# Two decoder blocks on one core: the embedding product, the gates and the stick attention in another order

## The reference

```
h = h + 0.5 * swiglu(rmsnorm(h, ffn2_norm), w_gate, w_up, w_down)     # "MLP 2"
gate = sigmoid(rmsnorm(h, ple_gate_norm) @ ple_w_gate)                 # 1024 x 1024
emb  = rmsnorm(p @ ple_w_proj, ple_norm)                               # p is 512 x 256: does not depend on h
h = h + gate * emb

mem_attention(rmsnorm(x), rmsnorm(mem, norm_mem), ...)                 # mem is 256 x 1024

# stick breaking, per head, strictly causal
z = q @ k.T / 8
log_beta, log_1m = log_sigmoid(z), where(strict, log_sigmoid(-z), 0)
tail = reverse_cumsum(log_1m) - log_1m
out = where(strict, exp(log_beta + tail), 0) @ v
```

## Time and profile before

| | |
|---|---|
| median of 3 executions | 2682.81 us |
| profiled execution | 2682.83 us, span 2680.9 |
| TensorE matmul busy | 2611.9 us (97%) |
| VectorE busy | 1567.8 us (58%) |
| ScalarE busy | 909.2 us (34%) |
| mean granted TensorE clock | 0.99 |
| load of a slab, issue to landing | 4.8 us |
| chain that ended last | 90% TensorE, 7% VectorE, 2% ScalarE |

### The profile page before, as it was taken

The page is one execution under the profiler, slowest core; times in us unless marked ns, Lnnn a source line. Parts: engine busy times, 40 slices in busy tenths (PEclk is TensorE's granted clock), DMA queues, the critical chain, the costliest instruction groups (busy, mean ns, idle before and its releaser), DMA issues.

```text
span 2680.9 us, 32197 instructions
## 1 busy us (share of the span) xinstructions
PE 2611.9 (97%) x12690; PEld 2140.0 (80%) x12690; DVE 1567.8 (58%) x1934; ACT 909.2 (34%) x1186; POOL 0.2 (0%) x4
## 2 busy tenths in 40 slices
PE   8999999989999999998999999999999999999999
PEld 6888887768888877876888888888886789888887
DVE  6444456676444468477555766566346656574745
ACT  4222243544212134434342423234136343432322
POOL 0000000000000000000000000000000000000000
PEclk9999999999999999999999999999999999999999
DMA  5222232003322222211322222323210132122222
GB/s 176 95 94 94 94 121 80 32 33 103 109 86 102 94 94 89 101 64 63 110 96 78 96 97 92 108 81 129 95 64 1 63 126 95 64 95 96 102 100 79
DMA packets 36596, 240.68 MB, mean 90 GB/s; under 512 B 3952, under 2 KB 6912, under 8 KB 8320
## 3 DMA queue, kind: packets, MB, share of 16 engines
q1 hardware_dynamic: 35008, 234.12, 25.4%
q10 hardware_dynamic: 1472, 4.94, 0.5%
HBM read 236.94 MB, written 2.10 MB: 89 GB/s over the span
## 4 chain that ended last, share of the span: by engine, by line
PE 90%; DVE 7%; ACT 2%; issue 1%; DMA 0%; SPq 0%; DVEq 0%; ACTq 0%
PE ps L474 24%; PE ps L476 24%; PE ps L475 24%; PE ps L1061 1%; PE ps L492 1%; PE ps L491 1%; PE ps L490 1%; PE ps L1007 1%; PE ps L502 1%; PE ps L1046 1%; PE ps L587 1%; DVE w_lo L1712 1%; PE ps L589 1%; PE ps L588 1%; PE ps L1072 1%
## 5 line engine op out<-in xcount | busy, mean ns | idle before, releaser
L474 PE MATMUL ps<-op_hi,w_hi 128*128 128x512 f32 x2128 | 841.3, 395 | 20.5 <-DVE op_lo L1626 14.5
L475 PE MATMUL ps<-op_lo,w_hi 128*128 128x512 f32 x2128 | 831.3, 391 | 0.0
L476 PE MATMUL ps<-op_hi,w_lo 128*128 128x512 f32 x2128 | 831.2, 391 | 0.0
L1115 ACT ACTIVATE w_hi<-w_raw 128x2048 fp32r<-128x2048 f32 x217 | 414.2, 1909 | 515.0 <-PE ps L476 355.3
L1712 DVE TENSOR_TENSOR w_lo<-w_raw,w_hi 128x2048 fp32r<-128x2048 f32 x217 | 497.1, 2292 | 50.6 <-ACT w_hi L1115 35.2
L474 PEld LDWEIGHTS ps<-op_hi,w_hi 128*128 128x128 f32 x2128 | 401.5, 189 | 111.8 <-issue 20.5
L475 PEld LDWEIGHTS ps<-op_lo,w_hi 128*128 128x128 f32 x2128 | 401.6, 189 | 87.5 <-issue 4.4
L476 PEld LDWEIGHTS ps<-op_hi,w_lo 128*128 128x128 f32 x2128 | 401.4, 189 | 84.2
L1677 DVE SCALAR_TENSOR_TENSOR x<-ps,x 128x512 f32<-128x512 f32 x134 | 92.6, 691 | 338.6 <-PE ps L476 320.9
L474 PE MATMUL ps<-h_hi,w_hi 128*128 128x512 f32 x692 | 273.4, 395 | 0.0
L476 PE MATMUL ps<-h_hi,w_lo 128*128 128x512 f32 x692 | 273.4, 395 | 0.0
(11 more groups left out here) (293 smaller groups left out, 3002.3 us busy)
## 6 DMA issues: line engine op xcount, KB each, us to landing
w_raw<-in_wstream_dram SPq DMA_DIRECT2D x217, 1024.0 KB, 4.8
w_raw<-in_wstream_dram SPq DMA_DIRECT2D x8, 256.0 KB, 7.9
x<-in_x_dram SPq DMA_DIRECT2D x4, 512.0 KB, 7.6
cr_m<-in_mem_dram ACTq DMA_DIRECT2D x2, 1024.0 KB, 4.7
out_dram<-x SPq DMA_DIRECT2D x3, 512.0 KB, 2.7
ev_s<-in_alibi_dram ACTq DMA_DIRECT2D x1, 1024.0 KB, 4.9
m_c<-in_rope_dram ACTq DMA_DIRECT2D x1, 704.0 KB, 4.3
pl_p<-in_p_dram ACTq DMA_DIRECT2D x1, 512.0 KB, 3.6
```

The source lines that it names most:

```text
L474: mm_(o, w_hi[:, c % 4, w], hi[:, k, 0:cols], start=(k == 0), stop=False)
L475: mm_(o, w_hi[:, c % 4, w], lo[:, k, 0:cols], start=False, stop=False)
L476: mm = mm_(o, w_lo[:, c % 4, w], hi[:, k, 0:cols], start=False, stop=(k == kt - 1))
L1115: f_(w_hi[:, c % 4, :], w_raw[:, c % 2, :], ACT.Copy).then_inc(w_hi_ready, 1)
```

## The change

- The embedding slab moves ahead of MLP 2's last four down slabs (`AT_EMB`), in the weight stream too. Its tiles go round five banks. ScalarE squares each tile in its bank and copies it to `pl_e` (`emb_kept`); VectorE copies only the eighth. Its row sum stands behind the first down slab. Embedding tiles 4 to 7 are scaled between down slabs, 0 to 3 between gates.
- A gate bank is freed when VectorE has scaled it, and the sigmoid waits for that. The last gate slab is made by halves. The order of the even mixer's norm is written out by tile.
- Memory's row sum stands behind the second slab of the even mixer's projection; `high(...+5)` goes ahead of `rs_mem`.
- Stick attention works in three units per pair, each with a pair of banks of its own: unit 0 is blocks 3 and 2 (384 columns), unit 1 block 1 (384), unit 2 block 0 (512). ScalarE and VectorE handle a unit with one instruction where they had one per block. Unit 0's buffers alternate between two sets. Units 0 and 1 of pair 0 are scored before the last value slab. The output takes blocks from 3 to 0 and waits per block. The projection's operand 0 to 6 is cut once the last exponent is made, and the eighth straight from its bank.

```diff
@@ TensorE
-            def mlp(at):
+            def embeddings(c):
+                start_slab(c)
+                pe.wait_ge(p_cut, 2)
+                for o in range(KT):
+                    if o >= 5:
+                        pe.wait_ge(emb_kept, o - 4)
+                    ...
+                    mm.then_inc(emb_done if o < KT - 1 else slab_done, 1)
+            def mlp(at, emb=False):
...
+                        if emb and d == 0:
+                            sum_rows(columns=False)
...
+                if emb:
+                    embeddings(AT_EMB)
...
-                    if memory and d == 0:
+                    if memory and d == 1:
                         sum_rows(MEM)
...
-            for d in range(1, DOWN):
-                to_features(AT_PLE + 1 + d, last=(d == DOWN - 1))
+            for d in range(1, DOWN - 1):
+                to_features(AT_PLE + d)
+            by_halves(AT_PLE + DOWN - 1, KT, gate_half, op_hi, op_lo, last=True)
...
+            def stick_scores(t, u):
+                if t:
+                    pe.wait_ge(a_made, 3 * (t - 1) + u + 1)
+                for kb in UNITS[u]:
+                    ...
+            stick_scores(0, 0)
+            stick_scores(0, 1)
+            to_positions(AT_ODD + ODD_SLABS - 1)
+            pe.wait_ge(acc_free, AT_ODD + ODD_SLABS + 1)
             for t in range(PAIRS):
-                stick_exponent(t, 3)
-                stick_scores(t, 1)
-                stick_scores(t, 0)
+                if t:
+                    stick_scores(t, 1)
+                stick_scores(t, 2)
                 if t:
                     stick_out(t - 1)
-                stick_exponent(t, 2)
+                stick_exponent(t, 0)
                 stick_exponent(t, 1)
                 if t < PAIRS - 1:
-                    stick_scores(t + 1, 3)
-                    stick_scores(t + 1, 2)
-                stick_exponent(t, 0)
+                    stick_scores(t + 1, 0)
+                stick_exponent(t, 2)
@@ ScalarE
+                if emb:
+                    high(AT_EMB + 3)
+                    for o in range(KT):
+                        ...
+                        square_sum(emb_bank(o))
+                        if o < KT - 1:
+                            f_(pl_e[:, o, :], emb_bank(o), ACT.Copy).then_inc(emb_kept, 1)
+                    high(AT_EMB + 4)
+                    high(AT_EMB + 5)
+                    inverse_rms_x(rs_emb, None)
+                    high(AT_EMB + 6)
...
+            for k in range(4):
+                act.wait_ge(gated_x, k + 1)
+                square_sum(x[:, k, :])
+            high(AT_EVEN + 2)
+            gate(KT - 2)
+            for k in range(KT - 1):
+                n["used"] += 1
+                act.wait_ge(op_used, n["used"])
+                if k == KT - 2:
+                    gate(KT - 1)
+                if k >= 4:
+                    act.wait_ge(gated_x, k + 1)
+                mixer_high(k)
...
             high(AT_EVEN + EVEN_SLABS + 4)
+            high(AT_EVEN + EVEN_SLABS + 5)
             inverse_rms_x(rs_mem, rs_col[:, NB:NB + 2])
-            high(AT_EVEN + EVEN_SLABS + 5)
...
+            soft(0, 0)
+            act.wait_ge(slab_done, AT_ODD + ODD_SLABS)
             for t in range(PAIRS):
-                weights(t, 3)
                 soft(t, 1)
-                soft(t, 0)
-                weights(t, 2)
+                soft(t, 2)
+                weights(t, 0)
                 weights(t, 1)
                 if t < PAIRS - 1:
-                    soft(t + 1, 3)
-                    soft(t + 1, 2)
-                weights(t, 0)
+                    soft(t + 1, 0)
+                weights(t, 2)
@@ VectorE
+                if emb:
+                    for o in range(KT):
+                        add_squares(o)
+                    v.tensor_copy(pl_e[:, KT - 1, :], emb_bank(KT - 1)).then_inc(acc_free, 1)
+                    low(AT_EMB + 3)
...
+            for k in range(4):
+                add_squares(k)
+            gate(KT - 2)
+            onto_x_gated(KT - 2)
+            for k in range(3):
+                low_part("mix0", k)
+            gate(KT - 1)
+            for k in range(3, KT - 1):
+                low_part("mix0", k)
+            onto_x_gated(KT - 1)
+            low_part("mix0", KT - 1)
+            for k in range(4, KT):
+                add_squares(k)
...
+            for d in range(4):
+                if d == 3:
+                    low(AT_ODD + 14)
+                    softplus(0, 0)
+                keep_rows(AT_ODD + 8 + d, ...)
             for t in range(PAIRS):
                 softplus(t, 1)
-                softplus(t, 0)
+                softplus(t, 2)
                 if t:
                     stick_out(t - 1)
                 if t < PAIRS - 1:
-                    softplus(t + 1, 3)
-                    softplus(t + 1, 2)
-            stick_out(PAIRS - 1)
-            dve.wait_ge(o_read, KT)
-            for t in range(KT):
+                    softplus(t + 1, 0)
+            dve.wait_ge(arg_ready, 3 * PAIRS)
+            for t in range(KT - 1):
                 operand(t, od_q[:, t, :])
+            dve.wait_ge(stick_ready, PAIRS)
+            operand(KT - 1, ps[:, stick_bank(PAIRS - 1), :])
```

More of the change, by code:

```diff
@@ L397, in keys_bank, with emb_bank, unit_bank, unit_z @@
             return 2 * (at % 2)
+        rs_emb = rs[:, 0, :]
+        def emb_bank(o):
+            b = pair_of(AT_EMB)
+            return ps[:, [b, b + 1, 5, 6, 7][o % 5], :]
         def query_bank(job):
             return 6 + job % 2
+        def unit_bank(u):
+            return [4, 6, pair_of(AT_ODD + ODD_SLABS - 2)][u]
+        def unit_z(u):
+            return ps[:, unit_bank(u):unit_bank(u) + 2, 0:UNIT_COLUMNS[u]]
+        def stick_bank(t):
+            return pair_of(AT_ODD + ODD_SLABS - 1) + t % 2
+        def unit_parts(t, u):
+            at, w = UNIT_AT[u], UNIT_COLUMNS[u]
+            if u == 0 and t % 2 == 0:
+                tiles = (od_s_even, od_hi_even, od_lo_even)
+            else:
+                tiles = (od_s, od_hi, od_lo)
+            return [tile[:, :, at:at + w] for tile in tiles]
         def spread(ap, n):
@@ L1029, in _ @@
                     sum_rows()
[L1030 removed]
+            for d in range(8, 11):
                 to_positions(AT_ODD + d)
[L1032 to L1044, removed]
[L1045 to L1051 removed]
@@ new lines, in _ @@
+            for k in range(4):
[11 more added lines that the diff above has]
+                mixer_high(k)
+            for k in range(4, KT - 2):
+                square_sum(x[:, k, :])
@@ L1446, in _ @@
+            act.wait_ge(gated_x, KT)
+            mixer_high(KT - 1)
+            for k in range(KT - 2, KT):
+                square_sum(x[:, k, :])
             logs_and_exps()
@@ L1713, in low, with update_and_norm @@
                                 ALU.subtract).then_inc(w_ready, 1)
-            def update_and_norm(c, name, scale=1.0, also=None, early=False, first=0):
+            def update_and_norm(c, name, scale=1.0, early=False, first=0, beside=None):
                 for d in range(DOWN - 1):
@@ L1720, in update_and_norm @@
                         low(c + d + 3)
+                    if beside is not None:
+                        beside(d)
                 def last():
                     onto_x(c + DOWN - 1, DOWN - 1, 0, scale)
-                    if also is not None:
-                        also()
                 if name is None:
@@ L2119, in _, with beside_down, gate @@
-            for d in range(DOWN - 1):
-                gate(d)
-                low(AT_PLE + 4 + d)
-            norm_x("mix0", lambda: gate(DOWN - 1))
+            def beside_down(d):
+                if d == 1:
+                    use_rs_x()
+                    dve.wait_ge(emb_kept, KT - 1)
+                    scale_embedding(range(4, KT))
+            mlp(AT_MLP2, "ple_gate", emb=True)
+            low(AT_PLE + 2)
+            use_rs_x()
+            low(AT_PLE + 3)
+            def gate(k):
+                c = AT_PLE + k // 2
+                if c == AT_EVEN - 1 and k % 2 == 0:
+                    dve.wait_ge(gate_half, 1)
+                else:
+                    dve.wait_ge(slab_done, c + 1)
+                signal = acc_free if k % 2 else gate_scaled
+                v.tensor_tensor(pl_g[:, k % 2, :], acc(c, k % 2), rs_x[:], ALU.mult).then_inc(signal, 1)
+                done(signal)
@@ new lines, in onto_x_gated @@
+            def onto_x_gated(k):
+                dve.wait_ge(gated, k + 1)
+                v.tensor_tensor(tmp[:], pl_g[:, k % 2, :], pl_e[:, k, :], ALU.mult).then_inc(v_step, 1)
+                done(v_step)
+                v.tensor_tensor(x[:, k, :], x[:, k, :], tmp[:], ALU.add).then_inc(gated_x, 1)
+                done(gated_x)
+            for d in range(DOWN - 1):
+                gate(2 * d)
+                gate(2 * d + 1)
+                if d < 2:
+                    scale_embedding((2 * d, 2 * d + 1))
+                onto_x_gated(2 * d)
```

(3 more changed lines are left out.)

280 lines of the change are left out of this document (125 added, 155 removed).

## The result

| kernel | median us (runs) | range |
|---|---|---|
| before | 2683.62 (4) | 2682.56 to 2686.56 |
| changed | 2644.69 (4) | 2642.30 to 2644.92 |

The ratio is 0.9851, 95% interval 0.9834 to 0.9868. The forecast was 2645.0, counted from the 2682.81 of the first three executions of the kernel before; with a fourth its median is 2683.62. The profiled execution took 2644.92 with a span of 2643.0, against 2680.9: 37.9 us of span to be found.

A forecast was written before the change was run, and what follows sets the result against it. TensorE, busy 97% of the span, bounds the kernel; only its 69 us of idle time and its half clock can be won. Gains 14.1 + 8.9 + 15.3 = 38.3 from 2682.81 give 2644.5, stated as 2645; range 2637 to 2660.

The forecast's parts named there:

- Part 1, the product: Embedding product moved ahead of MLP 2's down slabs: 10.85 us without a wait, in place of 18.8.
- T+4.8: T is the end of MLP 2's last up slab; ScalarE was forecast to start on the product's tiles at T+4.9.
- Rival D: Moved product not hidden: ScalarE takes over 1.36 us per tile, 7.95 us come back, 2653; chance 0.07.
- Part 1, the even entry: Gates' end before the even mixer: waits of 2.1 us in all, bounds 0 to 8.7; all of part 1 gains 14.1.
- the 1.4: Even entry: TensorE's wait at its row sum, as squares 4 to 7 are added until E+22.6.
- E+21.2: E is the last gate slab's start; TensorE was forecast to want its row sum 21.2 us later.
- Part 2: Memory's row sum moved one slab later in the even mixer's output: gain 8.9 us, bounds 5.5 to 9.0.
- Part 3: Stick attention in three units per pair, with early scores and new tail: gain 15.3 us, bounds 8.1 to 18.1.
- one wait of 1.65: Stick attention's start: TensorE waits 1.65 us ahead of exponent 1 of pair 0.
- rival B: Clock fall stays at the even entry or stick stage's start: about 3 us plus some 2 of wait; 2650, both 2654; 0.14.
- Rival A: Unit 2's chain of scores, softening and cuts bounds the stick stage: period 13.3, 2652; chance 0.12.
- Rival C: Stick stage keeps its start's half clock, its 99.6 us of work doubling: 2744, slower; chance 0.03.

The follow-up runs named there:

- runs 6 and 7: Changed kernel with unit 2's rounding copy in stick attention made one further time per pair (6), then three further times (7): 2645.76 and 2660.06 us.
- run 1: Changed kernel with memory's row sum back behind the first output slab and memory's rs ahead of the weight copy: 2652.29 us.

## Why the prediction was right, and where it was not

The sum was 38.3. The medians differ by 38.9 (2683.62 to 2644.69), or by 38.1 from the 2682.81 that the prediction started at; the two profiled executions differ by 37.9. The parts were less exact than that.

- **What bounds the kernel**: right. TensorE's idle time and half clock gave the whole gain, and the shorter work of the other engines none of it.
- **Part 1, the product (10.85, no wait)**: right in its place, banks, start of ScalarE (T+4.8) and absence of a wait. TensorE took 11.2, with 0.233 a matmul for the 0.226 of the down slabs. Too slow was ScalarE's pace, 1.25 forecast and 0.95 measured: I added recorded durations and a hand-over, but two operations of one queue start 0.47 apart. It cost the sum nothing. Rival D needed a pace over 1.36 and was farther off than I had put it; the experiment with two banks shows that ScalarE's late start, not its pace, is what the banks bridge. The table load's row (1.28, next operation at once) held. By the 2.66 us of the Trainium skill's page "ScalarE: Activation LUTs", "What ACT_TABLE_LOAD costs", an estimate puts tile 0's bank at T+7.6 and a wait of 0.8 on TensorE. The trace disagrees: ScalarE's copy of tile 0 ends at T+5.9, and there is no wait.
- **Part 1, the even entry (waits of 0.5 + 0.2 + 1.4)**: measured 0.18 in the timeline, none, and 0.17. The term that failed is the 1.4. I had TensorE at its row sum at E+21.2, though my own 10.9 + 0.5 and eight tiles of 1.36 end at E+22.3. The other failure is small: the first low part was ready earlier. The waits came out 1.75 shorter than forecast; the product and the slabs behind it were a little slower than 0.226 a matmul, and 0.9 beyond the 14.1 is left.
- **An unforecast 1.3** came at the even mixer's output, where the change does nothing. The 2.88 us wait there is the same in both traces; 6.7 us at half came with it before and 3.3 after. Over the ten traces that have this wait it is about 3.4 in five and 6.8 in five. I count it as chance. The prediction did not have this wait in its list of those behind which the clock falls.
- **Part 2 (8.9)**: right to a tenth in the traces (9.0 between before and after, and 9.0 in the run with the sum put back); 7.6 by the medians of that run. Nothing queued behind it was late, memory's rs included.
- **Part 3 (15.3)**: the period (12.45, measured 12.40), the first wait (1.65, measured 1.62), the tail wait (0.65, measured 0.81) and the vanished gap before the projection are as forecast. The gain in the two profiled executions is 12.6. The step that failed is "one wait of 1.65" counted as 1.65 alone: a half-clock stretch of 6.7 us stands behind it in this trace and costs 3.0. The prediction had named a fall of the clock where it has none as a sign of being wrong, and for this place it was. It is rival B's second half at B's 3 for the stretch, without the 2 of further wait that B added. Where it is absent (the changed kernel's second profile) the stage gains 15.7. The sum gave no reason for taking none here, though rival B names the 1.58 that came before one.
- **Rival A**: excluded by the periods of runs 6 and 7. The chain has some 0.8 to spare, 0.35 less than forecast. **Rival C**: excluded; the clock is 1.00 in every steady period, and the stretch ends by itself.
- **The balance**: 0.9 + 1.3 + 0.1 more than forecast, 2.7 less. With nothing else changed, the stretch's absence at the stick stage would have made it 2642; but in the one profiled execution without it the other stretches were longer, and it took 2646.50. The exactness of 0.3 us is luck: eight executions of the changed kernel lie between 2642.30 and 2646.50. The range and the mechanism are what the prediction earned.

Open: why the stretch comes behind the 1.62 us wait in one execution and not in another, and how long it lasts. The traces show only that both vary with nothing changed in the program. Part 3 was undone only as a whole: what the units, the early scores and the new tail give one by one is read from the waits that are gone, not shown by runs of their own. So is the new place of the product, whose banks alone were tested.

## What to carry to other kernels

Where one engine is busy all the time, find its waits one by one, and price each with the half-clock stretch that comes with it: here a wait of 5.5 costs some 9 and one of 1.6 costs 1.6 or 4.7, from one execution to another. When a sum rests on such stretches, say per wait with what chance one comes, instead of taking none.

Here banks, not speed, bridged a late consumer: with ScalarE free only 4.8 us into the product, five banks gave no wait, and two gave 2.8. And check the room in a chain by adding to it in two sizes, one below and one beyond: the one shows that the room is real, the other how large it is.

## What the runs showed of the hardware that was not expected

- ScalarE's operations of 512 columns from PSUM start every 0.47 us in a run of them, while each is recorded with 0.58 to 0.74. The recorded duration of one is not its share of the queue.
- The clock falls behind a wait of 1.62 us in five traces of eight, and stays at 1.00 behind the same wait in three, one of them of the same program. The same stage takes 116.6 or 113.5 accordingly (runs 6 and 7, with more VectorE work in the stage, are left out of these two figures). With the wait of 2.88 us at the even mixer's output it fell in each of the ten traces that have the wait, for about 3.4 or 6.8 us.
- In the longer waits the granted clock is at half before the wait ends: of the 5.42 us in run 1 the last 3.57 show 0.53. Behind 1.62 us the whole stretch stands behind the wait.
- Seven matmuls without use, in a wait that TensorE has anyway, cost nothing (113.55 for the stage, as in the execution without a fall).
